# Bias rows stored in eight pieces, one norm's scale loaded alone, and two groups of VectorE work moved, in a two-block transformer kernel

## What is computed

```
first block
  h = rms_norm(x, mix_pre_g);  proj = h @ w_in
  o_da = differential_attention(q, k, v)      8 heads, scores + rel_bias[bucket(distance)], causal
  o_hg = hgrn2(f, q, i, g)                    8 heads, gated linear attention with a decay
  x += rms_norm(concat(o_da, o_hg) @ w_out, mix_post_g)
  x += rms_norm(cross_attention(x, mem), cross_post_g)
  x += rms_norm((silu(gate) * up) @ w_ffn_out, ffn_post_g)
second block
  x += nsa_mixer(rmsnorm(x, mix_norm_g_2))    16 heads, bias by relative position, compressed keys
  x += swiglu(rmsnorm(x, ffn_norm_g_2));  return rmsnorm(x, final_norm_g_2)
```

## Time and profile before

| | |
|---|---|
| median of 3 runs | 2526.82 us (2526.11 to 2528.39) |
| the profiled execution's own time | 2535.6 us |
| its span | 2533.8 us |
| TensorE matmul busy | 2486.1 us, 98% |
| VectorE busy | 1424.4 us, 56% |
| ScalarE busy | 1220.1 us, 48% |
| moved by DMA | 456.17 MB, mean 180 GB/s |

### The profile page before, as it was taken

How to read it: one execution, slowest core, us unless ns; L and a number is a source line. 1 busy time by engine, 2 the same in 40 slices (tenths; PEclk the granted TensorE clock), 3 DMA queues, 4 the chain that set the end, 5 groups by cost and what they waited for, 6 DMA issues and landing times.

```text
span 2533.8 us, 32126 instructions
## 1 busy us (share of the span) xinstructions
PE 2486.1 (98%) x12059; PEld 2079.8 (82%) x12059; DVE 1424.4 (56%) x1926; ACT 1220.1 (48%) x1696; POOL 33.3 (1%) x50
## 2 busy tenths in 40 slices
PE   8979999999999999999999999999999999999998
PEld 6857888788888888888888898887888888888887
DVE  5537888776545554554446555676655544554444
ACT  5545446756544444444445555554544444444443
POOL 1000000000000000000000000000000000000000
PEclk9989999999999999999999999999999999999999
DMA  7756554454666666666665775343566666666564
GB/s 238 224 133 163 158 160 153 151 186 155 193 189 190 187 189 187 190 189 192 193 195 168 221 224 175 100 132 119 172 193 188 190 189 187 190 189 207 193 192 157
DMA packets 244197, 456.17 MB, mean 180 GB/s; under 512 B 21828, under 2 KB 30276, under 8 KB 243584
## 3 DMA queue, kind: packets, MB, share of 16 engines
q1 hardware_dynamic: 234896, 440.92, 57.4%
q0 software_dynamic: 9200, 13.88, 2.1%
HBM read 449.40 MB, written 5.24 MB: 179 GB/s over the span
## 4 chain that ended last, share of the span: by engine, by line
PE 92%; DMA 3%; DVE 3%; ACT 2%; issue 1%; POOL 0%; DVEq 0%; ACTq 0%; POOLq 0%
PE g L305 23%; PE g L307 23%; PE g L306 23%; PE g L1018 3%; PE g L1020 3%; PE g L1019 3%; DMA raw<-in_w_in 3%; PE g L1972 1%; PE g L1974 1%; PE g L1976 1%; PE m L1048 1%; DVE wl L293 1%; PE m L654 1%; PE m L752 1%; ACT wh L289 1%
## 5 line engine op out<-in xcount | busy, mean ns | idle before, releaser
L293 DVE TENSOR_TENSOR wl<-raw,wh 128x1024 fp32r<-128x1024 f32 (+1 forms) x836 | 1015.7, 1221 | 962.3 <-ACT wh L289 959.0
L289 ACT ACTIVATE wh<-raw 128x1024 fp32r<-128x1024 f32 (+1 forms) x836 | 879.5, 1056 | 1128.5 <-PE g L307 911.7
L305 PE MATMUL g<-wh,act_hi 128*128 128x512 f32 x1800 | 706.1, 392 | 4.7 <-DVE wl L293 4.3
L307 PE MATMUL g<-wh,act_lo 128*128 128x512 f32 x1800 | 701.2, 390 | 0.0
L306 PE MATMUL g<-wl,act_hi 128*128 128x512 f32 x1800 | 700.6, 389 | 0.0
L305 PEld LDWEIGHTS g<-wh,act_hi 128*128 128x128 f32 x1800 | 337.9, 188 | 75.9 <-DVE wl L293 6.0
L307 PEld LDWEIGHTS g<-wh,act_lo 128*128 128x128 f32 x1800 | 337.8, 188 | 71.1
L306 PEld LDWEIGHTS g<-wl,act_hi 128*128 128x128 f32 x1800 | 338.1, 188 | 68.6
L305 PE MATMUL g<-wh,ht_hi 128*128 128x512 f32 x672 | 261.6, 389 | 0.0
L307 PE MATMUL g<-wh,ht_lo 128*128 128x512 f32 x672 | 261.4, 389 | 0.0
L306 PE MATMUL g<-wl,ht_hi 128*128 128x512 f32 x672 | 261.4, 389 | 0.0
(11 more groups left out here) (381 smaller groups left out, 2341.6 us busy)
## 6 DMA issues: line engine op xcount, KB each, us to landing
raw<-in_w_ffn_in SPq DMA_DIRECT2D x176, 512.0 KB, 3.6
raw<-in_ffn_w_in SPq DMA_DIRECT2D x176, 512.0 KB, 3.7
raw<-in_w_in SPq DMA_DIRECT2D x112, 512.0 KB, 4.7
raw<-in_w_ffn_out SPq DMA_DIRECT2D x88, 512.0 KB, 4.3
raw<-in_ffn_w_out SPq DMA_DIRECT2D x88, 512.0 KB, 4.2
raw<-in_nsa_w_in SPq DMA_DIRECT2D x80, 512.0 KB, 4.3
raw<-in_w_out SPq DMA_DIRECT2D x32, 512.0 KB, 4.4
raw<-in_nsa_w_out SPq DMA_DIRECT2D x32, 512.0 KB, 4.5
```

The costliest lines, as they stand in the source:

```text
L289: nc.scalar.activation(wh[:, j % SLOTS, 0:n], raw[:, j % SLOTS, 0:n], ACT.Copy).then_inc(hi_done, 1)
L293: nc.vector.tensor_tensor(wl[:, j % SLOTS, 0:n], raw[:, j % SLOTS, 0:n], wh[:, j % SLOTS, 0:n].bitcast(F32), ALU.subtract).then_inc(lo_don ...
L305: nc.tensor.matmul(dst, h, whk, start=(first and k == 0), stop=False)
L307: ins = nc.tensor.matmul(dst, l, whk, start=False, stop=(last and k == 1))
```

## The change

It stores the bias rows in eight parts by row (all 24 heads, 16 rows each) in place of twelve parts by head, spaced four units apart; loads the first norm's scale alone, as the first transfer of SyncE's queue, and turns the other five later; loads x in eight pieces alternating with the first eight units; moves `dve_mh_rows(1)` and `dve_mh_rows(2)`, `(3)` on VectorE; turns the gelu one unit later on TensorE; and adds a finished output chunk ahead of the scores of the next step.

```diff
-        BIAS_PARTS = 12
+        BIAS_PARTS = 8
+        BIAS_ROWS = P // BIAS_PARTS
...
-            act.wait_ge(gains_ready, 1)
+            act.wait_ge(gains_ready, 1 if name == "n1" else 2)
...
-            "n1": (8, x_rows, lambda pe, b: pe.wait_ge(x_in[b // 2], 16)),
+            "n1": (8, x_rows, lambda pe, b: pe.wait_ge(x_in[b], 16)),
...
+            return {2: lambda: dve_other_gains(dve), 10: log_f(0), 11: log_f(1), 21: one_less_f(0), 22: one_less_f(1), 23: lambda: dve_lambda(dve),
...
+        def pe_other_gains(pe):
+            pe.wait_ge(gains_in, 16 * 5)
+            nc.tensor.transpose(m[:, 1, 0:6 * 16], g_rows[:, :], ident[0:6 * 16, 0:6 * 16]).then_inc(gains_turned, 1)
+
+        def dve_other_gains(dve):
+            dve.wait_ge(gains_turned, 2)
+            nc.vector.tensor_copy(g_cols[:, 16:96], m[:, 1, 16:96]).then_inc(gains_ready, 1)
+            dve.wait_ge(gains_ready, 2)
...
             dve_da_scores(dve, 0, 1)
+            dve_mh_rows(dve, 1)
             dve_mx_unit(dve, 70)
             dve_mem_lo(dve, 5)
-            dve_mh_rows(dve, 1)
...
-            for n in range(73, 76):
-                dve_mx_unit(dve, n)
+            dve_mx_unit(dve, 73)
+            dve_mx_unit(dve, 74)
+            for b in range(2, 4):
+                dve_mh_rows(dve, b)
+            dve_mx_unit(dve, 75)
...
-                if p == 1:
-                    for b in range(2, 4):
-                        dve_mh_rows(dve, b)
...
-                if n == NTH["vw", 2]:
+                if n == NTH["vw", 3]:
                     pe_turn_hidden(pe)
...
                 f = FILL + 6 * p
+                dve_in2_evict(dve, f - 1)
                 for l in LANES:
                     dve_scores(dve, p, l)
-                dve_in2_unit(dve, f + 3)
+                dve_in2_unit(dve, f + 3, evict=False)
...
+            sp.dma_start(g_rows[0:16, :], a["mix_pre_g"].rearrange("(k p) -> k p", p=P)).then_inc(gain_in, 16)
             sp.dma_start(ident[:, :], a["c_ident"]).then_inc(ident_in, 16)
...
-                sp.dma_start(x[:, :, n * NB:(n + 1) * NB], a["x"].rearrange("(t p) d -> p t d", p=P)[:, :, n * NB:(n + 1) * NB])\
+                sp.dma_start(x[:, :, n * HB:(n + 1) * HB], a["x"].rearrange("(t p) d -> p t d", p=P)[:, :, n * HB:(n + 1) * HB])\
...
-            x_cols(0)
-            in1f_unit(0)
-            in1f_unit(1)
-            x_cols(1)
-            in1f_unit(2)
-            in1f_unit(3)
-            x_cols(2)
-            x_cols(3)
-            sp_gemm(sp, "in1f", lambda c: c * NB + F_HG, done=SLOTS)
+            for n in range(8):
+                x_cols(n)
+                in1f_unit(n)
+            sp_gemm(sp, "in1f", lambda c: c * NB + F_HG, done=8)
...
-                pool.wait_ge(lo_done, SLOTS + in1q_0 + 22 + 3 * n)
-                rows = bt[2 * n:2 * n + 2, :]
-                skewed = bass.AP(tensor=rows.tensor, offset=rows.offset + P - 1, ap=[list(rows.ap[0]), [-1, P], [1, S]])
-                pool.dma_start(dram_bias[2 * n:2 * n + 2], skewed).then_inc(bt_stored, 16)
+                pool.wait_ge(lo_done, SLOTS + in1q_0 + 22 + 4 * n)
+                rows, r0 = bt[:, :], n * BIAS_ROWS
+                skewed = bass.AP(tensor=rows.tensor, offset=rows.offset + P - 1 - r0, ap=[list(rows.ap[0]), [-1, BIAS_ROWS], [1, S]])
+                pool.dma_start(dram_bias[:, r0:r0 + BIAS_ROWS, :], skewed).then_inc(bt_stored, 16)
...
-            pe.wait_ge(gains_in, 16 * 6)
-            nc.tensor.transpose(g[:, 2, 0:6 * 16], g_rows[:, :], ident[0:6 * 16, 0:6 * 16]).then_inc(gains_turned, 1)
-            pe.wait_ge(gains_ready, 1)
-            pe_gemm(pe, "in1f", turn="n1")
+            pe.wait_ge(gain_in, 16)
+            nc.tensor.transpose(g[:, 2, 0:16], g_rows[0:16, :], ident[0:16, 0:16]).then_inc(gains_turned, 1)
+            pe_gemm(pe, "in1f", turn="n1", also={12: lambda: pe_other_gains(pe)})
```

More of the change, by code:

```diff
@@ L231, in build @@
         tables_in, ident_in = sem("tables_in"), sem("ident_in")
-        x_in = [sem(f"x_in{n}") for n in range(4)]
+        x_in = [sem(f"x_in{n}") for n in range(8)]
         ga_in, gb_in, bias_in = sem("ga_in"), sem("gb_in"), sem("bias_in")
-        gains_in, gains_turned, gains_ready = sem("gains_in"), sem("gains_turned"), sem("gains_ready")
+        gain_in, gains_in, gains_turned, gains_ready = sem("gain_in"), sem("gains_in"), sem("gains_turned"), sem("gains_ready")
         chain_a, chain_d, chain_p = sem("act_step"), sem("dve_step"), sem("pool_step")
@@ L611, in act_lead_in @@
                     if name == "n1":
-                        for c in range(4):
+                        for c in range(8):
                             act.wait_ge(x_in[c], 16)
@@ L911, in one_less_f @@
                 return step
-            return {10: log_f(0), 11: log_f(1), 21: one_less_f(0), 22: one_less_f(1), 23: lambda: dve_lambda(dve),
+            return {2: lambda: dve_other_gains(dve), 10: log_f(0), 11: log_f(1), 21: one_less_f(0), 22: one_less_f(1), 23: lambda: dve_lambda(dve),
                     28: lambda: dve_var(dve, "nmem"), 30: lambda: dve_rstd(dve, "nmem")}
+        def pe_other_gains(pe):
[5 more added lines that the diff above has]
+            dve.wait_ge(gains_ready, 2)
         def dve_lambda(dve):
@@ L2244, in dve_in2_evict, with dve_in2_unit @@
             nc.vector.tensor_tensor(xc, g[:, 2 * (c % 2):2 * (c % 2) + 2, :], xc, ALU.add).then_inc(pair_free[c % 2], 1)
-        def dve_in2_unit(dve, n):
+        def dve_in2_unit(dve, n, evict=True):
             dve_unit(dve, in2_0 // SLOTS, n, 192 if ORDER[n][0] == "gl" else UE)
-            dve_in2_evict(dve, n - 4)
+            if evict:
+                dve_in2_evict(dve, n - 4)
         def dve_sum_block(dve, b):
@@ L2414, in _ @@
         def _(pool):
-            for n, k in enumerate(("mix_pre_g", "mem_norm_g", "cross_pre_g", "ffn_pre_g", "mix_norm_g_2", "ffn_norm_g_2")):
-                pool.dma_start(g_rows[16 * n:16 * n + 16, :], a[k].rearrange("(k p) -> k p", p=P)).then_inc(gains_in, 16)
+            for n, k in enumerate(("mem_norm_g", "cross_pre_g", "ffn_pre_g", "mix_norm_g_2", "ffn_norm_g_2")):
+                pool.dma_start(g_rows[16 * n + 16:16 * n + 32, :], a[k].rearrange("(k p) -> k p", p=P)).then_inc(gains_in, 16)
             pool.dma_start(tab[0:32, 0:8], a["rel_bias"]).then_inc(tables_in, 16)
@@ L2529, in _ @@
             dve.wait_ge(gains_turned, 1)
-            nc.vector.tensor_copy(g_cols[:, :], g[:, 2, 0:6 * 16]).then_inc(gains_ready, 1)
+            nc.vector.tensor_copy(g_cols[:, 0:16], g[:, 2, 0:16]).then_inc(gains_ready, 1)
             dve.wait_ge(gains_ready, 1)
```

## The result

| | before | after |
|---|---|---|
| median of the runs, us | 2527.61 (2526.11 to 2529.18, 4 runs) | 2496.56 (2495.77 to 2497.39, 4 runs) |
| profiled execution, own time | 2535.6 | 2496.48 |
| its span, mean granted clock | 2533.8, 0.992 | 2494.7, 0.998 |

The changed kernel takes 0.9877 of the time before, with an interval of 0.986 to 0.9894: 31.0 us less by the medians, 39.1 by the profiled executions. The forecast was 2495 us, faster.

What follows compares the result with a forecast made beforehand. TensorE was busy for 98% of the span, so only its waits and slow stretches could be won: 28.8 + 1.8 + 2.7 + 2.4 = 35.7 us. That gave 2499.9 or 2491.1; the middle, 2495 us, was forecast, range 2487 to 2508.

Steps and rivals of the forecast that it cites:

- The bound: Whole kernel: TensorE has matmuls for 98% of the span, so only its standing still or running slowly can be won.
- Bias rows, 28.8: Stage from 113 to 260 us: the old store's late weight loads cost 29.8 us; 28.8 won, 1 us left as residue.
- near 167: Sign in the profile after: copy L1304 of the first head comes near 167 us, down from 191.8.
- Start, 1.8: Start of the kernel: no wait for six scales, first product at 9.2 us instead of 12.06; 1.8 us won.
- the start does not get earlier: Rival, chance 0.06: smaller x pieces run slower, one is late; the 1.8 goes, up to 2 us lost, 2499 us.
- The estimate of 20.8 us for eight pieces one after another: Within the start rival: 8 x 2.6 us instead of 4 x 3.2 = 12.8, and the kernel at 2505 us.
- Differential attention, 2.7: Differential attention: moving `dve_mh_rows` into VectorE's gaps removes TensorE's waits of 2.3 and 1.3 us; 2.7 us won.
- Second mixer, 2.4: Second mixer: the later gelu covers 0.9 us, the earlier chunk addition removes waits of 3 x 0.5; 2.4 us won.
- The 8.8 us that the profiled execution had over its median: Excess before: if it lies elsewhere, runs give 2491.1 us; if in the loads the store delays, 2499.9; middle taken, 2495.
- Twelve engines crowded: Rival, chance 0.12: weight loads and store parts share engines for most of each spacing; half of 29.8 stays, 2509 us.
- Still two engines: Rival, chance 0.05: the new store parts still run on two engines, the loss stays at 29.8, 2524 us.
- The store stops all loads: Rival, chance 0.03: the write to DRAM sets the store's rate; each of eight parts holds all loads, 2600 us.

Runs made afterwards that it cites:

- no_bias: The changed kernel with the bias rows stored as before, in twelve parts by head: 2520.55 us, ratio 0.9972.
- bias_only: The kernel before with only the new store of bias rows, eight parts by row: 2503.14 us, ratio 0.9882.
- half_rows: The kernel before with each of its twelve store parts halved: 24 parts of two heads and 64 rows; 2536.1 us, ratio 1.0028.
- four_heads: The kernel before with its store in six parts of four heads every six units, not twelve of two every three: 2578.19 us, ratio 1.0193.

## Why the prediction was right, point by point

**The bound.** Right: with the late loads the waits for `wl` and `dec` and the slow clock went together, and nothing else became the bound.

**Bias rows, 28.8.** The size of the loss, 29.8, is confirmed in the profiled execution (31.1), by three pieces added up; the residue of 1 us was none. The new part's cost was mis-sized, 47.7 us of engine time against 19 measured, because it was scaled by bytes; loads beside it landed in 4.4 us, not in up to 8.5, and were not held at all. The rule of the Trainium skill, DMA: Bandwidth & Descriptors, section "Why a DMA increments its semaphore by 16 and not by 1", gave 2 and 12 engines, and for four heads it gives 4. The traces agree: two, twelve and four packets of the store were in progress at once. With the rule went the expectation that parts of four heads are cheaper, and that was wrong by 60 us. So the forecast was right on twelve engines, and right that two are dear; why they are dear is not explained by it. The first head's copy at 166.78 for "near 167" is partly luck: up to it 24.6 us came back, not 23.3, and the start gave 0.35, not 1.8.

**Start, 1.8.** The step that failed. The first product came as forecast, and the term counted that as won. It is given back at unit 2, whose load lands at least 2.0 us later than before (the start is worth 0.1 us measured by leaving it out, 0.35 in the changed kernel's trace). The forecast followed the chain to the first unit only, and took fewer bytes in the queue for an earlier landing. The rival "the start does not get earlier" is what happened, at its milder end. The estimate of 20.8 us for eight pieces one after another and 2505 in all, worked out from a page of the Trainium skill, was not seen: x is not waited for beyond 3.5 us. That page, DMA: Bandwidth & Descriptors, gives its fixed 2.0 us in the section "Anatomy of one DMA — SWDGE (gpsimd) path", for transfers that GpSimd issues, and x is loaded by SyncE.

**Differential attention, 2.7.** Measured 3.1 together with the start (2503.14 less 2499.99) in runs, 3.0 in the traces. The waits that went and the two that came (0.8 and 1.3) are those that the text names.

**Second mixer, 2.4.** Measured 3.1 to 3.4. The waits of 1.5 and 0.9 went whole; 0.8 more came behind the last scores, and their source was not followed up.

**The 8.8 us that the profiled execution had over its median.** The forecast took the middle between two readings. The runs speak for the second: with the old store sets of 7 to 25 runs spread over 9 to 16 us (2517.24 to 2532.4 in no_bias), with the new one, spaced or doubled, sets of four runs over 1 to 3, and a profiled execution's time less its loss in the stage is the same again (2535.6 - 31.1 = 2504.5 before, 2503.8 in bias_only). So the excess most likely lay in the very loads that the store delays, both fall to one floor, and the runs gain the 24.3 us of bias_only; the runs without a profile have no trace that would show it. By that reading the sum gave 2499.9, 3.3 above the result, and by the middle 2495, 1.6 below. That the middle came nearer is luck. The sum of 35.7 fell 3.4 short of the 39.1 of the profiled executions: it had 1.5 too much for the start, but 2.3 too little for the store, 1.3 too little for differential attention and the second mixer, and nothing for the 1.2 of a stretch of slower clock that the profile before happened to have. The middle then took off another 4.9 us for a reading that the runs speak against, and this made up for the shortfall.

**Rivals.** Twelve engines crowded: no, even at twice the store. Still two engines: no. The store stops all loads: not when spaced; issued at once it delays them once, for 5 to 6 us.

## What to carry to other kernels

When weight loads are late beside another transfer, compute the pace that their landing allows, (landing + turnaround) over the number of buffers, against the time of a unit. Here that came within 9 us of the loss of six kernels, though it missed the 5 us of a single burst; the other queue's share of the engines (24.6% in half_rows, 18.2% in four_heads, which lost more than twice as much) does not tell it. Lay a background store out so that each piece spans many partitions, as the parts over 24 did here, and space the pieces. To measure parts worth 1 to 3 us, take each out of the version whose runs agree, and follow an earlier start at least as far as the first load that the earlier work catches up with.

## What the runs showed of the hardware that was not expected

- A store of 256 KB from two partitions took 31.8 us of engine time, one of 384 KB from 24 partitions 19 us: 2.5 times less for each byte. The old part had 528 packets and the new one 154, but most of the difference lies in the packets of 4096 bytes, 0.42 us each against 0.17.
- A store from four partitions, 512 KB, took 26.5 us to land, longer than the 15.8 of 256 KB from two, and held weight loads for 19.3 us; the kernel was 51 us slower.
- Halving the parts to 128 KB halved their landing (8.2 us) and raised the engine time recorded from 16.2% to 24.6%, with loads no faster (12.3 us).
- Parts of 2, 4 and 24 heads had two, four and twelve packets in progress at once.
- Kernels in which the two queues contend also scatter: those with parts of two heads spread over 9 to 16 us (7 to 25 runs each), those with row parts over 1 to 3 (4 runs each).
- The new start moved 270 GB/s from 2 to 12 us where the old one moved 310, and the third weight unit landed at least 2.0 us later with 248 KB less ahead of it in its queue.
